# Narrow products of the large expert turns in four column groups, and a ring place loaded only after TensorE is done with it

## What is computed

```python
def moe_swiglu(x, w_router, b_router, w_gate, w_up, w_down):
    logits = (x @ w_router + b_router).astype(jnp.float32)
    top_v, top_i = lax.top_k(logits, TOP_K)          # 2 of 8 experts
    ...
    for e in range(N_EXPERTS):
        out = out + gates[..., e:e + 1] * swiglu(x, w_gate[e], w_up[e], w_down[e])

def swiglu(x, w_g, w_u, w_d):
    return (jax.nn.silu(x @ w_g) * (x @ w_u)) @ w_d
```

## Time and profile before

| | us |
|---|---|
| median of 3 runs | 1990.87 |
| the profiled execution | 1984.89 |
| its span | 1983.1 |
| turns, by ScalarE's first instruction of each | 1023.8, then 1187.3, 1288.8, 1388.7, 1488.7, 1588.6, 1688.5, 1788.4 |
| last matmul of the last turn starts | 1950.9 |

### The profile page before, as it was taken

How to read it: one execution, slowest core, us unless ns; L and a number is a source line. 1 busy time by engine, 2 the same in 40 slices (tenths; PEclk the granted TensorE clock), 3 DMA queues, 4 the chain that set the end, 5 groups by cost and what they waited for, 6 DMA issues and landing times.

```text
span 1983.1 us, 28034 instructions
## 1 busy us (share of the span) xinstructions
PE 1878.6 (95%) x10353; PEld 1604.9 (81%) x10354; DVE 1482.1 (75%) x2119; ACT 1066.3 (54%) x1206; POOL 136.5 (7%) x159
## 2 busy tenths in 40 slices
PE   7999999899998999999889999999999999999993
PEld 7899899799987989899766678888888888886672
DVE  6997686755536999667576668888888888886665
ACT  4452754543324444474444456767777776765442
POOL 1110000000001020000020001020202020201000
PEclk9999999899999999999989999999999999999997
DMA  7553344344443563444456569898989898996522
GB/s 268 203 215 143 138 151 144 109 168 149 149 141 116 191 229 136 149 149 150 149 211 250 199 233 339 335 382 331 374 331 380 337 375 333 366 346 241 210 106 87
DMA packets 118613, 446.91 MB, mean 225 GB/s; under 512 B 10384, under 2 KB 10384, under 8 KB 118016
## 3 DMA queue, kind: packets, MB, share of 16 engines
q1 hardware_dynamic: 112288, 424.45, 58.1%
q0 software_dynamic: 6240, 21.33, 3.2%
HBM read 435.68 MB, written 12.67 MB: 226 GB/s over the span
## 4 chain that ended last, share of the span: by engine, by line
PE 42%; issue 3%; DVE 3%; ACT 1%; DMA 1%; SPq 0%; DVEq 0%; POOLq 0%; POOL 0%; ACTq 0%
PE psum L1996 11%; PE psum L1997 11%; PE psum L1998 11%; PE psum L2003 3%; PE psum L2002 3%; ACT wph L616 1%; PE psum L1736 1%; PE psum L2059 1%; DVE wpl L622 1%; DVE hT L1674 0%; DMA x<-out_acc 0%; DMA out_acc<-arena,rows_out 0%; DVE arena L1663 0%; PE psum L2062 0%; DVE x L1164 0%
## 5 line engine op out<-in xcount | busy, mean ns | idle before, releaser
L622 DVE TENSOR_TENSOR wpl<-e_ring,wph 128x2048 fp32r<-128x2048 f32 x269 | 606.9, 2289 | 85.5 <-ACT wph L616 84.5
L616 ACT CAST wph<-e_ring 128x2048 fp32r<-128x2048 f32 x269 | 501.7, 1903 | 119.6 <-PE psum L1998 66.7
L574 DVE TENSOR_TENSOR wl<-ring,wh 128x1024 fp32r<-128x1024 f32 x234 | 285.3, 1223 | 208.1 <-ACT wh L568 207.4
L1750 PE MATMUL psum<-xTh,wh 128*128 128x320 f32 x1184 | 375.3, 317 | 31.6 <-DVE xTl L1266 11.0
L1751 PE MATMUL psum<-xTl,wh 128*128 128x320 f32 x1184 | 369.9, 312 | 0.0
L1752 PE MATMUL psum<-xTh,wl 128*128 128x320 f32 x1184 | 369.7, 312 | 0.0
L568 ACT CAST wh<-ring 128x1024 fp32r<-128x1024 f32 x234 | 243.9, 1046 | 138.6 <-PE psum L1771 71.2
L1996 PE MATMUL psum<-wph,xe 128*128 128x512 f32 (+1 forms) x768 | 293.6, 382 | 2.8 <-issue 2.4
L1997 PE MATMUL psum<-wph,xe 128*128 128x512 f32 (+1 forms) x768 | 289.1, 376 | 0.0
L1998 PE MATMUL psum<-wpl,xe 128*128 128x512 f32 (+1 forms) x768 | 288.7, 376 | 0.0
L1750 PEld LDWEIGHTS psum<-xTh,wh 128*128 128x128 f32 x1184 | 225.7, 191 | 40.0 <-DVE wl L574 15.7
(11 more groups left out here) (327 smaller groups left out, 2528.5 us busy)
## 6 DMA issues: line engine op xcount, KB each, us to landing
e_ring<-experts SPq DMA_DIRECT2D x264, 1024.0 KB, 6.4
ring<-stream SPq DMA_DIRECT2D x274, 512.0 KB, 3.2
lnp<-rows POOLq DMA_DIRECT2D x4, 1024.0 KB, 6.1
x<-x POOLq DMA_DIRECT2D x3, 512.0 KB, 5.8
arena<-x0T SPq DMA_DIRECT2D x2, 640.0 KB, 5.9
o_a<-arena POOLq DMA_DIRECT2D x2, 540.0 KB, 7.6
o_k<-arena POOLq DMA_DIRECT2D x2, 512.0 KB, 7.0
o_v<-arena POOLq DMA_DIRECT2D x2, 512.0 KB, 8.8
```

What stands on the lines that cost most here:

```text
L574: dve.tensor_tensor(wl[:, q % SPLITS, :], ring[:, u % SLOTS, :], wh[:, q % SPLITS, :].bitcast(F32), ALU.subtract).then_inc(lo_done, 1)
L616: act.copy(wph[:, SLOT_OF[m % NPOS], :], ring_place(m).rearrange("p u c -> p (u c)")).then_inc(hi_e, 1)
L622: dve.tensor_tensor(wpl[:, s, :], ring_place(m).rearrange("p u c -> p (u c)"), wph[:, s, :].bitcast(F32), ALU.subtract).then_inc(lo_e, 1)
L1750: pe.matmul(out, h[:, k], hi[:, k], start=(k == 0), stop=False)
```

## The change

Large turns: B is computed with exact float32 products. x and hidden rows of B are kept unsplit (`xe_b`, `hT_b`), the moving operand is the raw weight in `e_ring`, and four products with 32 stationary columns write four groups of 32 PSUM partitions (`GROUPS` = 4): for gate and up, one group per block of 128 weight columns; for down, one per 256 output columns. The steps on ScalarE and VectorE that joined the halves of B go, and those left work on 128 x 128 or 128 x 256 tiles instead of 32 x 512. The share and the row number of B are made for all four groups (`choose`: four products where one was, in every turn), and B is scattered as 128 rows of 256.

All turns: since `e_ring` is now read by TensorE, SyncE waits for `mm_e` (TensorE done with the position) instead of `lo_e`. Loads are issued in the order in which places come free.

```diff
+FIRST_LOADS = [m for m in range(LOAD_AHEAD) if SLOT_OF[m] not in SLOT_OF[:m]]
+TURN_LOADS = sorted((m for m in range(2 * NPOS) if 0 <= before_in_slot(m) < NPOS and SLOT_OF[m % NPOS] in SLOT_OF[:m]),
+                    key=before_in_slot)
+LAST_LOADS = [m for m in TURN_LOADS if m < NPOS]
...
-            def expert(i, e, last):
-                for m in range(LOAD_AHEAD, last):
-                    sp.wait_ge(lo_e, i * NPOS + (before_in_slot(m) + 1))
+            def expert(i, e, loads):
+                for m in loads:
+                    sp.wait_ge(mm_e, i * NPOS + (before_in_slot(m) + 1))
                     load(m, e + 1 if m >= NPOS else e)
...
# ScalarE and VectorE, large turns
-                        act.copy(gate_b[0:CAP_B, 0:w], psum[CAP_B:2 * CAP_B, BANK_X, 0:w])
+                        act.activation(sg_b[0:rows], psum[0:rows, BANK_X, 0:P], ACT.Sigmoid)
-                def up_chunk(j):
...
-                    act.activation(sg_b[0:CAP_B, 0:w], gate_b[0:CAP_B, 0:w], ACT.Sigmoid)
-                    act.copy(h_b[0:CAP_B, 0:w], psum[CAP_B:2 * CAP_B, BANK_T, 0:w]).then_inc(hb_ready, 1)
...
-                        dve.tensor_tensor(gate_b[0:CAP_B, 0:w], gate_b[0:CAP_B, 0:w], sg_b[0:CAP_B, 0:w], ALU.mult)
-                        dve.tensor_tensor(h_b[0:CAP_B, 0:w], psum[0:CAP_B, BANK_T, 0:w], h_b[0:CAP_B, 0:w], ALU.add)\
...
+                        dve.tensor_tensor(h_b[0:rows, 0:P], psum[0:rows, BANK_T, 0:P], sg_b[0:rows], ALU.mult)
...
-                if big:
-                    dve.wait_ge(ys_done, i * 2 + 2)
-                    for c in range(2):
-                        dve.tensor_tensor(ys_b[0:CAP_B, 512 * c:512 * c + 512], psum[0:CAP_B, BANK_DB + c, :],
...
-                    dve.tensor_scalar(ys_b[0:CAP_B], ys_b[0:CAP_B], gate_out[0:CAP_B, 1:2], None, ALU.mult)
...
+                    act.activation(ys_b, psum[:, BANK_DB, 0:D_OF], ACT.Copy, scale=gate_out[:, 1:2])
...
# TensorE: choose, every turn
-                    ins = product(chosen[0:CAP_B, 3:6], pick[:, t, P:CAP], values[:, t, :], t, 3)
+                    for g in range(GROUPS):
+                        ins = product(chosen[CAP_B * g:CAP_B * g + CAP_B, 3:6], pick[:, t, P:CAP], values[:, t, :],
+                                      t, 3)
...
# TensorE: gate and up of B
-                        ins = packed(b, slice(0, 2 * P * n), xe[:, k, BOTH_B], xe[:, k, HI_B], h[:, :, ks],
-                                     low[:, :, ks], k == 0, k == KT - 1)
+                        for g, w in enumerate(weight):
+                            ins = pe.matmul(psum[CAP_B * g:CAP_B * g + CAP_B, b, 0:P], xe_b[:, k],
+                                            w[:, P * k:P * k + P], start=(k == 0), stop=(k == KT - 1),
+                                            skip_group_check=True)
...
# TensorE: down of B, once for every 128 hidden columns
-                                ins = packed(BANK_DB + c, slice(0, 512), th[:, BOTH_B], th[:, HI_B], h[:, u, cs],
-                                             low[:, u, cs], False, final)
+                        for g in range(GROUPS if big else 0):
+                            ins = pe.matmul(psum[CAP_B * g:CAP_B * g + CAP_B, BANK_DB, 0:D_OF],
+                                            th_b,
+                                            ring_place(AT["down", f])[:, u, D_OF * g:D_OF * g + D_OF],
+                                            start=False, stop=final, skip_group_check=True)
...
# TensorE: turning the hidden rows of B
-                        for n in range(nf):
-                            ins = pe.transpose(psum[:, BANK_U, CAP_B * n:CAP_B * n + CAP_B],
-                                               h_b[0:CAP_B, P * n:P * n + P], ident[0:CAP_B, 0:CAP_B])
+                        rows = CAP_B * nf
+                        ins = pe.transpose(psum[:, BANK_U, 0:rows], h_b[0:rows, 0:P], ident[0:rows, 0:rows])
```

More of the change, by code:

```diff
@@ L131, in fills_of @@
     return sum(s == slot for s in SLOT_OF[:n])
+FIRST_LOADS = [m for m in range(LOAD_AHEAD) if SLOT_OF[m] not in SLOT_OF[:m]]
+TURN_LOADS = sorted((m for m in range(2 * NPOS) if 0 <= before_in_slot(m) < NPOS and SLOT_OF[m % NPOS] in SLOT_OF[:m]),
+                    key=before_in_slot)
+LAST_LOADS = [m for m in TURN_LOADS if m < NPOS]
+assert sorted(LAST_LOADS + FIRST_LOADS) == list(range(NPOS)) and len(TURN_LOADS) == NPOS
+assert sorted(m - NPOS for m in TURN_LOADS if m >= NPOS) == FIRST_LOADS
 assert len(SLOT_OF) == NPOS
@@ L448, in trunk @@
         hT = place("hT", [P, 2, 4, 2 * CAP], xtl_at, F32R)
+        xe_b = place("xe_b", [P, KT, 2 * CAP], xth_at)[:, :, ALL_B]
+        hT_b = place("hT_b", [P, 2, 4, 2 * CAP], xtl_at)[:, :, :, ALL_B]
         xT = place("xT", [P, KT, T], xtl_at)
@@ L1125, in turn @@
                         gate_chunk(j)
-                    if big and kind == "up" and ends:
-                        up_chunk(j)
                     expert_hi(act, n + SPLIT_AHEAD, i)
@@ L1151, in _ @@
         def _(dve):
-            for _ in range(24):
+            for _ in range(20):
                 dve.sem_inc(dve_placed, 1)
@@ L1639, in gate_chunk @@
                     if big:
-                        dve.tensor_tensor(gate_b[0:CAP_B, 0:w], psum[0:CAP_B, BANK_X, 0:w], gate_b[0:CAP_B, 0:w],
-                                          ALU.add)
+                        rows = w // GROUPS
+                        dve.tensor_tensor(sg_b[0:rows], psum[0:rows, BANK_X, 0:P], sg_b[0:rows], ALU.mult)
                     sg = sg_e if big else h_b
@@ L1998, in triple @@
                     return pe.matmul(out, hi, low, start=False, stop=final, skip_group_check=True)
-                def packed(bank_b, cs, both, hi, h, low, first, final):
-                    pe.matmul(psum[0:2 * CAP_B, bank_b, cs], both, h, start=first, stop=final, skip_group_check=True)
-                    return pe.matmul(psum[0:CAP_B, bank_b, cs], hi, low, start=False, stop=final,
-                                     skip_group_check=True)
                 def into(kind, j, b, at, halfway=None):
@@ L2043, in down @@
                     for u in range(2):
-                        th = hidden[:, 2 * (f % 2) + u]
+                        th, th_b = hidden[0][:, 2 * (f % 2) + u], hidden[1][:, 2 * (f % 2) + u]
                         final = f == FT // 2 - 1 and u == 1
@@ L2082, in turn @@
                         pe.wait_ge(idx_done, i + 2)
-                        into_b("gate", 1, BANK_X, at)
+                        into_b("gate", 1, BANK_X)
                         pe.wait_ge(htl_done, done + 1)
@@ L2086, in turn @@
                     if big:
[L2087 removed]
+                        into_b("up", 1, BANK_T)
                     else:
@@ L2090, in turn @@
                     for f in CHUNKS[0]:
-                        down(f, at, hT[:, 0])
+                        down(f, at, (hT[:, 0], hT_b[:, 0]))
                 last = i * NJ + (NJ - 1)
@@ L2096, in turn @@
                 if big:
-                    into_b("gate", NJ - 1, BANK_X, begin)
+                    into_b("gate", NJ - 1, BANK_X)
                     pe.wait_ge(htl_done, last)
@@ L2107, in turn @@
                 turn_hidden(2, last + 1)
-                down(FT // 2 - 2, begin, hT[:, 0])
+                down(FT // 2 - 2, begin, (hT[:, 0], hT_b[:, 0]))
                 rows_turned(i + 1, 1)
@@ L2114, in turn @@
                     pe.wait_ge(htl_done, last + 1)
-                down(FT // 2 - 1, begin, hT[:, 1])
+                down(FT // 2 - 1, begin, (hT[:, 1], hT_b[:, 1]))
             turns(pe, turn)
```

111 lines of the change are left out of this document (42 added, 69 removed).

## The result

The changed kernel takes 2160.34 us, the median of 4 runs (2156.91 to 2167.68), against 1989.99 (1988.71 to 1992.35) before: 1.086 times as long, 95% interval 1.083 to 1.089. The way was forecast, the size was not: 2060, with a range up to 2108.

A forecast was written before the change was run, and what follows sets the result against it. TensorE was taken to bound every small turn with next to no slack. Terms -40 - 2.7 + 4 + 88 + 13.5 + 6 = +69 on 1984.9 gave 2054, with 6 for the median 2060 us; range 2030 to 2108.

The forecast's parts named there:

- B: Large turns, narrow products in column groups on TensorE: -19.8 us per turn, -40 for both, and -2.7 once at the end.
- Rival D: Large turns: the column groups do not overlap here, +81 us per turn, 2222 us in all; chance 0.04.
- `choose`: Small turns, fourfold selection products on TensorE: 18 more records at 38 ns, 0.7 us per turn, +4.2 for six.
- Ring in small turns: Loads issued only when TensorE is done make three places wait for landings: 14.6 us per turn, +88 for six.
- Down 8 to down 10: Small turns: position 35's load, issued at down 8's end, delays hidden rows for down 10, no slack: +5.3 us per turn.
- Chunk 0 to chunk 1: Small turns: position 5's load, issued at gate's end, delays VectorE's selection and TensorE's `choose`: +4.5 us per turn.
- Gate pairs: Small turns, chunks 2, 3, 4 and last gate: load-to-low-part chain of 12.4 against 11.2 us, +1.2 each, +4.8 per turn.
- Clock: TensorE's clock falls after the wait at `choose` in half of seven turns, 1.7 us lost each: +6 (0 to +24).
- Rival C: TensorE's clock falls at both waits in every turn: 18 us more than forecast, 2078 us; chance 0.10.
- Ring in large turns: No wait between gate pairs; waits around chunk 0's `choose` and hidden rows, others at the ends: +13.5 us (+5 to +20).
- Rival A: Small turns: the loads stay hidden and the kernel is faster, 1966 us if they pay nothing; chance 0.08, of it 0.07 faster.
- Rival B: Loads come in bursts and the DMA is the bound, second landings of 9.4 us: +41, 2101 us; chance 0.14.

The follow-up runs named there:

- e2: Changed kernel with loads waiting for VectorE's low part as before, and B reading only the high part of the weights: 1956.74 us, ratio 0.983.
- e6: Kernel of e4, but in small turns the one load behind down 8 (position 35) waits for TensorE: 2044.42 us, ratio 1.027.
- e3: Changed kernel with the hidden rows' step and tile 0's turned rows ahead of the split of a newly loaded position on ScalarE and VectorE: 2079.58 us, ratio 1.047.
- e5: Changed kernel with filler products of zeros on TensorE ahead of three waits of each small turn: 2131.01 us, ratio 1.071.
- e1: Kernel before, B computed as before, with only the changed load lists and the wait for TensorE in every turn: 2192.88 us, ratio 1.102.
- e4: Changed kernel with loads waiting for TensorE only in large turns, for VectorE's low part in small ones: 1998.55 us, ratio 1.004.
- e10: Changed kernel with selection and hidden-row work ahead of the splits, and small-turn loads waiting for VectorE's low part: 1961.32 us, ratio 0.986.
- e11: Kernel of e2 with B's gate and up loops exchanged, one column group after another: 2037.65 us, ratio 1.024.

## Why the prediction was right or wrong

**B: right.** "Net -19.8 per turn", -40 for both: 20.6 + 20.6 = 41.2 measured by e2 against before. At the end of the program another 2.7 was forecast; from the end of the last turn to the end of the span it is 28.2 before and 26.3 in e2, 1.9 less. Together 42.7 forecast, 43.1 measured. The row of the attention scores gave the price of a form that the kernel's turns did not yet have. (34 bursts at 0.22 are 7.5, not 6.8; this changes little.) Rival D is out.

**`choose`: wrong and small.** +4.2 forecast for six turns. The rows of e2 show 0.16 per turn, and the length of a turn at most 0.1. The price came from records in one column group, and the new ones go to four; that this is the reason was not tested for products this small.

**Ring in small turns: right mechanism, waits left out.** "Sum: 5.3 + 4.5 + 4.8 = 14.6 per small turn, six turns = +88". Measured are 775.9 - 613.3 = 162.6 (table, after against e2), of which 109.8 are idle time of TensorE and 52.8 are longer busy time, nearly all of which belongs to the clock below. So 88 stands against 110. Term by term in the fifth turn:
- Down 8 to down 10: 5.3 forecast, 5.45 measured; alone in e6, 5.4 to 5.7.
- Chunk 0 to chunk 1: 4.5 forecast, 5.54 measured. The load of position 5 landed 6.3 us after its issue, not 5.1; the scatter of the turn before still took about half of the DMA engines' time until 1598, 2 us into that load.
- Gate pairs: 4.8 forecast, 2.37 + 0.83 + 0.77 + 0.59 = 4.6 measured. That the sum fits is partly luck, for it was to be 1.2 four times. The second landings of the last three came 7.4 to 7.5 after the first issue, near; that of the first came 9.1 after it (0.6 between the issues and 8.5, the longest of the row below), while the rows of the next turn were being gathered on the same DMA engines.

```profile
L687 SPq DMA_DIRECT2D e_ring<-experts x2: 372/372/373, 1617.7 to 1618.4; - x2
...
DMA to landing us min/median/max: 4.9/6.7/8.5
```

- "Three places matter" failed: 3.12 + 1.73 us stand at two more. In both a step on the hidden rows is queued behind a split that waits for a landing. The text looked at what stands behind the split of positions 5 and 35, and only there; "downs wait for nothing" was said of the weights and overlooked that the hidden rows for down 8 stand behind position 32's split.

**Clock: the term that failed most.** "If the clock falls in half of seven turns, at 1.7 us lost each: +6" against 9.7 us in one small turn, some 53 in six. The step that failed is the weighing: the price of half clock was counted for half of the turns and one wait of 1.7 us in each; the trace after has four falls in the fifth turn, some 2.4 us each. In the trace after the clock is at 0.50 after each of the two waits over 5 us, and after those of 3.12 and 2.37 us as well. No length decides by itself: after 2.38 us in e3 (at 1642.19) it stayed at 1.00, and after the 2.36 us of the kernel before too. Rival C had the right kind of cost and less than half of its size (24 us against 53). The row that the term rests on was also weaker than it was read: the products ahead of that gap started 0.27 apart, just as those behind it, though the granted clock is given as 1.00 there (kernel before, TensorE in order of time).

```profile
9.73 0.47 PE L1750 MATMUL psum<-xTh,wh 128*128 128x320 f32 x1
10.00 0.47 PE L1751 MATMUL psum<-xTl,wh 128*128 128x320 f32 x1
...
15.24 0.47 PE L1750 MATMUL psum<-xTh,wh 128*128 128x320 f32 x1
15.50 0.47 PE L1751 MATMUL psum<-xTl,wh 128*128 128x320 f32 x1
```

The Trainium skill ("TensorE: Matmul & The Clock Gate", "HAM oscillation") describes a kernel whose waits for data make TensorE start its next products at the lower clock. The trace after agrees, with 0.50 behind four waits of a turn. e5 shows what it costs here: 29 us come back for products of zeros.

**Ring in large turns: wrong.** "From gate pair to gate pair there are over 15 us, so no wait there", +13.5 in all. Measured 30.7 + 16.0 = 46.7 (after against e2). There is indeed no wait for a gate pair; the wait is ahead of up, for hidden rows behind the split of the second down position, 1.7 to 4.6 each (one 0.9), and 6.41 at `choose` in the first turn (expected 2.1 + 2.7). With the old B the same semaphore cost 21.0 + 15.5 (e1); probably a shorter B leaves less time under which a landing can hide.

**Not in the prediction:** turn 2 begins with 6 to 12 us of idleness in the versions with column groups (2.36 before), and the small turns of e2 are 12.3 longer together for it. And the turns start 4.6 us later than before; why was not followed up.

The sum closes: -41.2 + 162.6 + 46.7 + 12.3 + 4.6 - 2.2 (behind the last turn) = 182.8, as the spans: 2165.9 - 1983.1 = 182.8. The forecast was 69. Of the 114 that are missing the clock in small turns is the largest part (47), then the large turns (33), the idle time in small turns (22) and what the prediction did not have (17); smaller terms that went the other way take 5 off. Rival A is out. Rival B is right for a part only: in the fifth turn the second load of a pair landed 9.0 to 10.1 us after the first issue for four of ten pairs, all in the first third of the turn, and 7.4 to 7.8 for the other six. As the main cause it is out, since reordering (e3) freed 81 us at the same traffic.

## What to carry to other kernels

A semaphore that releases a buffer later puts a whole landing into the path of every engine that handles that buffer in a fixed order; list what stands behind each such step, for every position, and move the work that does not need the landing ahead of it. Where TensorE is the bound, price an idle stretch of some microseconds as the stretch and the half-clock products behind it, which here are a third of a small turn's loss (9.7 of 29.5 us). And make the costly wait conditional: it was needed in two turns of eight. Only with both is the kernel faster than before: the conditional wait alone gave 1998.55 us, the orders alone 2061.7, the two together 1961.32 against 1989.08 before.

## What the runs showed of the hardware that was not expected

- Float32 products with 32 stationary columns and 128 moving ones start 30 ns apart when consecutive ones go to four column groups (1.89 us for 64 records) and about 90 when they stay in one (5.96 us, less a tail of 0.27).
- Float32 products with 3 moving columns cost 0.16 us in all when 18 records are added in other column groups (e2 against before).
- Filler products of zeros hold the granted clock up: over the fifth turn it is 0.96 in e5 and 0.92 in the changed kernel.
- Two loads of 1 MB issued 0.6 us apart: the second landed 7.4 to 7.8 us after the first issue for six of ten pairs, and 9.0 to 10.1 in the first third of a turn, where a scatter, a gather or other loads were on the way (the changed kernel's fifth turn).
- The first small turn behind a large one starts with TensorE idle for 11.58 us (e2) or 6.41 us (e4), with no releaser in the profile. The programs with column groups fetch more instructions (64 packets on queue q8, 53 before). In that idle time, or just ahead of it, two packets of q8 come together (e2: 1173.7 to 1175.9), and TensorE starts 3.2 to 3.9 us after they end, in e2, e3, e4, e10, e11, the changed kernel and the kernel before (2.36 idle). In e1 three come one by one and there is no such idle time. This points at instruction fetches, but no run changed them alone, so the cause stays open.
